# Key-page products on VectorE instead of GpSimd, in a one-core hybrid decoder step

## The chip, the cores and the metric

One core of a Trainium2 chip runs the whole program in one launch. The metric is the device time in microseconds (us), median of three runs.

## The reference, cut to what matters

One layer of a decoder serves a prompt of 512 tokens and a group of 8 samples, one token each, with the same weights. The normalised rows go through one wide projection `w_in`, whose columns feed four branches (a short gated convolution A, a gated DeltaNet B, a Conformer convolution C, a forgetting attention D); gated, merged and projected by `w_out`, they are followed by cross attention and a convolutional FFN. The change is in branch D of the samples: each of the 8 samples attends to 2048 cached tokens, kept as 16 pages of 128 tokens, 128 pages in all, found through a page table:

```python
s = jnp.einsum('bqhd,bkhd->bhqk', qi, k, preferred_element_type=F32) * (d ** -0.5)
s = s + jnp.swapaxes(ci, 1, 2)[..., None] - ck
```

With one query token per sample, the first line is, for each page of 128 tokens by 8 heads by 64 channels, an elementwise product with the sample's query row (512 numbers) and a sum over the 64 channels of each head.

## The kernel before

Every weight matrix is cut into pieces of 128 columns (`PIECES`). For each piece SyncE loads the weights (`weights`, four pieces ahead, ring of five), ScalarE rounds them to a high half `wh`, GpSimd subtracts to get the low half `rawl` (`split`, L762, two pieces ahead), and TensorE forms three products, high by high, high by low and low by high, into one of two PSUM buffers `pb`. A piece is run in two halves of 260 tokens. VectorE or ScalarE then empties the buffer (`evac`); the pieces of kind `gx` are convolved by VectorE in that step (L1519, L1536, L1542, L1522).

The order of the work is one list, `TIMELINE`, made in Python by `timeline()`. Every engine walks the same list and issues its own share of each event, in that order, so an event that one engine must wait for delays all that this engine has behind it. Between the halves of pieces the list holds side items (`SIDE`: softmax rows, DeltaNet chunks `gdn`, layer norm `cln`, page logits `dc`, `ds`, ...), and three background streams, dealt out a few at a time by `background(kind, n)`: 124 convolution taps of branch C (`tap`, VectorE, L1648), 128 key pages (`k`), and value pages (`v`). After each half piece the loop calls `background("tap", ...)` and then `background("k", ...)`, with n of 1 or 2. A stream whose counter is still `None`, or at its end, adds nothing. The side list has marks: at `("REDUCES",)`, just after the third DeltaNet chunk and before the page logits, `background("k", 10 ** 6)` puts all pages not yet dealt out into the list at one place, and `kend` behind them.

A key page goes through a ring of four buffers `kring`. At event `k` i SyncE waits for `page_free` of page i-1 and loads page i+3 (`page`, L700 and L701); GpSimd multiplies page i by the query row `qb` (`product`, L773), which it has itself fetched from DRAM at every sixteenth page (L770); VectorE sums page i-1 over the heads' channels (`reduce_page`, L1655). At `kend` GpSimd fetches the pages' forget gates (L784), and the side item `dc` 0 sums them on VectorE (L1528) for TensorE. Helpers `tt`, `stt`, `ts` on VectorE issue an operation and wait for it before the next one. `own_head`, `qscr`, `qs_out` are the head mask, the queries in DRAM and the semaphore of their store.

Of the kernel before, what the change touches and what calls it, by code (L numbers as in the profile page):

```python
# [22 lines left out]
P = 128  # L23
# [191 lines left out]
def timeline():  # L215

    out, pos, step_n, tile, at_piece, bg = [], [0], [0], [0], [-1], {"tap": None, "k": None, "v": None}
    size = {"tap": N_TAP, "k": N_PAGE, "v": len(V_EVENTS)}

    def background(kind, n):  # L220
        for _ in range(n):
            if bg[kind] is not None and bg[kind] < size[kind]:
                out.append(V_EVENTS[bg[kind]] if kind == "v" else (kind, bg[kind]))
                bg[kind] += 1

# [206 lines left out]
def build(nc, a, out):  # L432
    ctx = ExitStack()
    with ctx:
# [225 lines left out]
        @block.sync  # L660
        def _(sp):
            sp.dma_start(cst[:, 0:2 * P], a["cst"][:, 0:2 * P]).then_inc(id_in, 16)
            for t in range(QT):
                sp.dma_start(xrow[:, t, :], a["x_prompt"][0, t * P:(t + 1) * P, :]).then_inc(x_in, 16)
            sp.dma_start(xrow[0:NB, QT, :], a["x_sample"].rearrange("b t d -> (b t) d")).then_inc(x_in, 16)
            sp.dma_start(cst[:, 2 * P:], a["cst"][:, 2 * P:]).then_inc(par_in, 16)
            sp.wait_ge(pool_made.sem, 1)
            rows = [(V_MIX, "norm_mix"), (V_CROSS, "norm_cross"), (V_FFN, "norm_ffn"), (V_MEM, "norm_mem"),
                    (V_CB, "conf_dw_b"), (V_LG, "conf_ln_g"), (V_LB, "conf_ln_b"), (V_GN, "gdn_norm")]
            for at, name in rows:  # L670
                src = a[name].rearrange("l (r c) -> (l r) c", c=P)
                sp.dma_start(pv[at:at + src.shape[0], B_VEC, :], src).then_inc(par_in, 16)
            sp.dma_start(pv[V_FIN:V_FIN + 8, B_VEC, :], a["norm_final"].rearrange("(r c) -> r c", c=P)).then_inc(par_in, 16)
            for at, b, name in ((V_SW, B_VEC, "sconv_w"), (V_GW, B_VEC, "gdn_conv_w"), (0, B_CW, "conf_dw_w"),
                                (0, B_FW, "ffn_conv_w")):
                src = a[name].rearrange("l w (r c) -> (l w r) c", c=P)
                sp.dma_start(pv[at:at + src.shape[0], b, :], src).then_inc(par_in, 16)
            for b, n, name in ((B_SS, 1, "state_sconv"), (B_GS, 4, "state_gdn_conv"), (B_CS, 8, "state_conf_conv"),
                               (B_FS, 4, "state_ffn_conv")):
                src = a[name].rearrange("b l w (r c) -> (b l w r) c", c=P)  # L680
                m = src.shape[0] // n
                sp.dma_start(pv[0:m, b:b + n, :], src.rearrange("(n m) c -> m n c", n=n)).then_inc(par_in, 16)
            with nc.allow_non_contiguous_dma(reason="16 columns of w_in, and vectors read by all partitions"):
                sp.wait_ge(pool_made.sem, 2)
                sp.dma_start(bias[:, 0:4], a["gdn_dt_bias"].to_broadcast([P, 4])).then_inc(small_in, 16)
                sp.dma_start(bias[:, 8:16], a["fox_fbias"].to_broadcast([P, 8])).then_inc(small_in, 16)
                sp.dma_start(bias[:, 16:20], a["gdn_a_log"].to_broadcast([P, 4])).then_inc(small_in, 16)
            def weights(p):

                u, half = PIECES[p][:2]  # L690
                w, row, kt, c = UNITS[u]
                c += half * P
                if p >= RING:
                    sp.wait_ge(piece_done.sem, p - RING + 1)
                sp.dma_start(raw[:, p % RING, 0:kt, :], W[w][row:row + kt * P, c:c + P].rearrange("(k p) n -> p k n", p=P))\
                    .then_inc(raw_in[p % RING], 16)

            def page(cache, i, to, landed):

                n = sp.value_load(ptr_[0:1, i:i + 1], min_val=0, max_val=a[cache].shape[0] - 1)  # L700
                sp.dma_start(to, a[cache][bass.ds(n, 1)].rearrange("a p l h d -> (a p) (l h d)")).then_inc(landed, 16)  # L701

            def k_page(i):
                page("cache_fox_k", i, kring[:, i % 4, :], page_in[i % 4])

            def v_group(g):
                for i in range(VG * g, VG * g + VG):
                    page("cache_fox_v", i, v_slot(i), v_in[i % 8])

            for p in range(RING - 1):  # L710
                weights(p)
            sp.wait_ge(pt_in, 32)
            for i in range(3):
                k_page(i)
            for e in TIMELINE:
                if e[0] == "piece" and e[2] == 0 and e[1] + RING - 1 < NP_:
                    weights(e[1] + RING - 1)
                elif e[0] == "k" and e[1] + 3 < N_PAGE:
                    if e[1] >= 1:
                        sp.wait_ge(page_free.sem, e[1])  # L720
                    k_page(e[1] + 3)
                elif e[0] == "vstart":

                    sp.wait_ge(pe_s.sem, upto(pe_works, ITEMS.index(("dc", 1)) + 1))
                    sp.wait_ge(sp_lo.sem, KB)
                    v_group(0)
                elif e[0] == "v" and VG * (e[1] + 1) < N_PAGE:
                    if e[1] >= 1:
                        sp.wait_ge(v_used.sem, e[1])
                    v_group(e[1] + 1)  # L730

            sp.dma_start(out["sc_s"][:, 0, 0:SCW - 2], a["state_sconv"][:, 0, 1:]).then_inc(out_sem, 16)
            sp.dma_start(out["gc_s"][:, 0, 0:GCW - 2], a["state_gdn_conv"][:, 0, 1:]).then_inc(out_sem, 16)
            sp.dma_start(out["cf_s"][:, 0, 0:CFW - 2], a["state_conf_conv"][:, 0, 1:]).then_inc(out_sem, 16)
            sp.dma_start(out["ff_s"][:, 0, 0:FCW - 2], a["state_ffn_conv"][:, 0, 1:]).then_inc(out_sem, 16)
# [3 lines left out]
        def _(pool):  # L739
# [22 lines left out]
                pool.tensor_tensor(rawl[:, p % RING, 0:kt, :], raw[:, p % RING, 0:kt, :],  # L762
                                   wh[:, p % (AHEAD + 1), 0:kt, :].bitcast(F32), SUB).then_inc(lo.sem, 1)

            def product(i):

                if i % PAGES == 0:
                    if i == 0:
                        pool.wait_ge(qs_out, 16)
                    pool.dma_start(qb[:, :], qscr[i // PAGES:i // PAGES + 1, :].to_broadcast([P, 512])).then_inc(qb_in, 16)  # L770
                    pool.wait_ge(qb_in, 16 * (i // PAGES + 1))
                pool.wait_ge(page_in[i % 4], 16 * (i // 4 + 1))
                own(pool.tensor_tensor(kring[:, i % 4, :], kring[:, i % 4, :], qb[:, :], MUL), prod_done)  # L773

            for p in range(AHEAD):
                split(p)
            for e in TIMELINE:
                if e[0] == "piece" and e[2] == 0 and e[1] + AHEAD < NP_:
                    split(e[1] + AHEAD)
                elif e[0] == "k":  # L780
                    product(e[1])
                elif e[0] == "kend":
                    pool.wait_ge(page_free.sem, N_PAGE)
                    pool.indirect_dma_start(lf[:, :, :].rearrange("p a b -> p (a b)"), None,  # L784
                                            a["cache_fox_logf"].rearrange("n p l h -> n (p l h)"),
                                            bass.IndirectOffsetOnAxis(ap=ptc[:, 0:1], axis=0)).then_inc(lf_in, 16)
                elif e[0] == "side" and e[2] == ("x", 0):

                    pool.wait_ge(qs_out, 32)
                    pool.wait_ge(mt_act.sem, mt_a[mt_of("cq")])  # L790
                    pool.dma_start(qx[:, :, :].rearrange("p b n -> p (b n)"),
                                   qscr.rearrange("b n -> (b n)")[None, :].to_broadcast([P, NB * 512])).then_inc(q8_in, 16)
                    pool.wait_ge(q8_in, 16)
                    pool.wait_ge(mk_in, 16)
                    for b in range(NB):
                        kprod.by(pool.tensor_tensor(kvc[:, b, :, :], kvc[:, b, :, :], spread(qx[:, b, :], 2, 1), MUL))
# [713 lines left out]
        def _(dve):  # L1510
# [140 lines left out]

            def reduce_page(i):

                dve.wait_ge(prod_done.sem, i + 1)
                page_free.by(dve.tensor_reduce(sc[:, i, :], kring[:, i % 4, :].rearrange("p (h d) -> p h d", h=FH), AX, ADD))  # L1655

            def side(K, s):
# [282 lines left out]
            for e in TIMELINE:  # L1940
# [20 lines left out]
                    tap(e[1])  # L1961
                elif e[0] == "piece" and e[2] == 0 and e[1] + AHEAD < NP_:
                    split(e[1] + AHEAD)
                elif e[0] == "k" and e[1] > 0:
                    reduce_page(e[1] - 1)
                elif e[0] == "kend":
                    reduce_page(N_PAGE - 1)
                elif e[0] == "v" and e[1] % V_OF == V_OF - 1:
                    dve.wait_ge(v_used.sem, e[1] + 1)
                    v_rows.by(dve.tensor_tensor(vdiag.rearrange("p (h d) -> p h d", h=FH), s3.rearrange("p (h d) -> p h d", h=FH),  # L1970
# [39 lines left out]
```

## Time and profile before

| what | value |
|---|---|
| median of 3 runs | 1837.2 us (1836.98 to 1845.5) |
| profiled execution | 1836.28 us |
| its span in the trace | 1834.5 us |
| TensorE, VectorE, GpSimd, ScalarE busy | 84%, 50%, 35%, 30% of the span |
| granted TensorE clock, mean | 0.893 |

The span is the time between the first and the last instruction that the trace holds; the execution's own time is 1.8 us longer. Busy shares are means over stretches that differ: which engine is full must be read stretch by stretch. In the trace PE is TensorE, DVE VectorE, ACT ScalarE, POOL GpSimd, SP SyncE, and `ar` is one large buffer that holds most intermediate tiles, the key pages and the query row among them.

### The profile page before, as it was taken

How to read it: one execution, taken by the hardware profiler on the slowest of the kernel's cores; microseconds unless marked ns; L12 is line 12 of the kernel's file. 1: busy time of each engine (PE TensorE's matmuls, PEld its weight loads, DVE VectorE, ACT ScalarE, POOL GpSimd, SP SyncE). 2: the span in 40 equal slices, each digit the busy share in tenths (PEclk: the TensorE clock that was granted, in tenths of full speed). 3: DMA queues.
4: the chain of work that ended last, by engine and by line, in shares of the span. 5: the costliest groups of instructions: out<-in, count | busy, mean ns of one | idle time of the engine just before them, and what ended most of it. 6: DMA issues, size and time to landing. Idle time of an engine off the chain costs nothing. (4 is left out here: it accounts for less than half of the span.)

```text
span 1834.5 us, 28395 instructions
## 1 busy us (share of the span) xinstructions
PE 1545.2 (84%) x11127; PEld 1426.6 (78%) x11127; DVE 917.6 (50%) x1353; ACT 555.8 (30%) x893; POOL 643.9 (35%) x354
## 2 busy tenths in 40 slices
PE   4996577789796978999888879889577999999996
PEld 3896577579796977877666659888476999999995
DVE  4169887998956743113222232264425566663122
ACT  3322441112214212254222223444214333333222
POOL 1266544555664712222111104310402344443440
PEclk8898787899898989999889879999867999999998
DMA  7145323433353416447433106432312233332331
GB/s 213 48 132 155 110 81 98 134 103 114 110 149 104 129 51 199 143 146 227 119 110 116 41 13 195 131 92 81 121 46 75 81 93 93 93 93 77 96 99 47
DMA packets 250997, 199.86 MB, mean 109 GB/s; under 512 B 11620, under 2 KB 208797, under 8 KB 250456
## 3 DMA queue, kind: packets, MB, share of 16 engines
q1 hardware_dynamic: 234149, 169.47, 31.7%
q10 hardware_dynamic: 15723, 23.86, 3.8%
q0 software_dynamic: 992, 4.72, 0.7%
q8 instruction: 88, 1.44, 0.3%
q14 instruction: 45, 0.37, 0.1%
HBM read 187.89 MB, written 10.81 MB: 108 GB/s over the span
## 5 line engine op out<-in xcount | busy, mean ns | idle before, releaser
L762 POOL TENSOR_TENSOR rawl<-raw,wh 128x1024 fp32r<-128x1024 f32 (+2 forms) x196 | 428.6, 2188 | 1040.4 <-ACT wh L1145 1038.8
L802 PE MATMUL pb<-xh,wh 128*128 128x260 f32 x2176 | 649.9, 299 | 48.7 <-DVE xl L1516 22.6
L802 PE MATMUL pb<-xl,wh 128*128 128x260 f32 x2176 | 633.7, 291 | 0.0
L802 PE MATMUL pb<-xh,rawl 128*128 128x260 f32 x2176 | 632.0, 290 | 0.0
L802 PEld LDWEIGHTS pb<-xh,wh 128*128 128x128 f32 x2176 | 430.7, 198 | 65.9 <-issue 39.2
L802 PEld LDWEIGHTS pb<-xl,wh 128*128 128x128 f32 x2176 | 430.5, 198 | 0.7
L802 PEld LDWEIGHTS pb<-xh,rawl 128*128 128x128 f32 x2176 | 429.9, 198 | 0.0
L1145 ACT ACTIVATE wh<-raw 128x1024 fp32r<-128x1024 f32 (+2 forms) x208 | 201.6, 969 | 551.1 <-PE pb L802 521.7
L802 PE MATMUL sd<-ar 128*128 128x128 f32 (+5 forms) x1584 | 280.9, 372 | 96.2 <-DVE ar L1516 37.2
L802 PEld LDWEIGHTS sd<-ar 128*128 128x128 f32 (+4 forms) x1584 | 200.2, 199 | 142.0 <-issue 80.8
L773 POOL TENSOR_TENSOR ar<-ar 128x512 f32<-128x512 f32 x128 | 187.5, 1465 | 86.3 <-DMA ar<-in_cache_fox_k 58.5
L1648 DVE SCALAR_TENSOR_TENSOR ar<-xT,cols,ar 128x512 f32<-128x512 f32 x120 | 134.5, 1152 | 1.2
L802 PE MATMUL pb<-oh,wh 128*128 128x260 f32 (+1 forms) x384 | 123.4, 321 | 7.6 <-ACT ar L1145 5.1
L802 PE MATMUL pb<-ol,wh 128*128 128x260 f32 (+1 forms) x384 | 117.0, 305 | 0.0
L802 PE MATMUL pb<-oh,rawl 128*128 128x260 f32 (+1 forms) x384 | 116.8, 304 | 0.0
L806 PE MATMUL sd<-cst,ar 128*128 128x128 f32 (+7 forms) x359 | 64.2, 302 | 51.0 <-DVE ar L1516 26.4
L1655 DVE TENSOR_REDUCE ar<-ar 128x8 f32<-128x512 f32 x128 | 84.7, 677 | 39.6 <-POOL ar L773 38.9
L802 PE MATMUL pb<-hh,wh 128*128 128x260 f32 x352 | 100.0, 284 | 2.6 <-DVE hl L1516 2.6
L1145 ACT ACTIVATE ar<-ar 128x520 f32<-128x520 f32 (+8 forms) x71 | 41.6, 586 | 195.3 <-DVE ar L1542 166.9
L802 PE MATMUL pb<-hh,rawl 128*128 128x260 f32 x352 | 99.5, 283 | 0.0
L802 PE MATMUL pb<-hl,wh 128*128 128x260 f32 x352 | 99.3, 282 | 0.0
L802 PE MATMUL sd<-ar,cst 128*128 128x260 f32 (+7 forms) x132 | 43.9, 473 | 65.1 <-DVE ar L1720 27.7
(168 smaller groups left out, 1739.6 us busy)
## 6 DMA issues: line engine op xcount, KB each, us to landing
raw<-in_w_in SPq DMA_DIRECT2D x80, 512.0 KB, 4.1
ar<-in_cache_fox_k SPq DMA_DIRECT2D x128, 256.0 KB, 2.7
ar<-in_cache_fox_v SPq DMA_DIRECT2D x128, 256.0 KB, 3.1
raw<-in_w_ffn_in SPq DMA_DIRECT2D x44, 512.0 KB, 3.7
raw<-in_w_branch SPq DMA_DIRECT2D x32, 256.0 KB, 3.2
raw<-in_w_ffn_out SPq DMA_DIRECT2D x16, 512.0 KB, 3.9
ar<-in_cache_mem_k ACTq DMA_DIRECT2D x1, 4096.0 KB, 19.5
raw<-in_w_out SPq DMA_DIRECT2D x8, 512.0 KB, 3.9
```

Source lines behind the costliest of these rows:

```text
L762: pool.tensor_tensor(rawl[:, p % RING, 0:kt, :], raw[:, p % RING, 0:kt, :], wh[:, p % (AHEAD + 1), 0:kt, :].bitcast(F32), SUB).then_inc(lo ...
L773: own(pool.tensor_tensor(kring[:, i % 4, :], kring[:, i % 4, :], qb[:, :], MUL), prod_done)
L802: return pe.matmul(o, l, r, start=start, stop=stop, skip_group_check=True)
L806: return pe.transpose(o, i, ident[0:n, 0:n])
L1145: own(act.activation(o, i, f, **kw), st)
L1648: dve_c.by(dve.scalar_tensor_tensor(out=oC[:, c, 0:SEQ], in0=g[:, j - 1:j - 1 + SEQ], scalar=w[:, j - 1:j], in1=oC[:, c, 0:SEQ], op0=MUL, ...
L1655: page_free.by(dve.tensor_reduce(sc[:, i, :], kring[:, i % 4, :].rearrange("p (h d) -> p h d", h=FH), AX, ADD))
```

## The change

GpSimd's `product` goes, with its query fetch. VectorE multiplies page i itself and sums it in the same event `k` i (before, it summed page i-1 there). SyncE fetches the query rows: the first at `kstart`, the next ones at the last page of each sample, once VectorE has made that page's product. And `background` gets a flag `turned`, by which the list leaves out one call for pages at each change of sample.

```diff
+    turned = [False]
     def background(kind, n):
         for _ in range(n):
             if bg[kind] is not None and bg[kind] < size[kind]:
+                if kind == "k" and bg[kind] % PAGES == 0 and bg[kind] > 0 and not turned[0] and n < 10:
+                    turned[0] = True
+                    return
+                turned[0] = False
                 out.append(V_EVENTS[bg[kind]] if kind == "v" else (kind, bg[kind]))
                 bg[kind] += 1
...
+            def query(b):
+                sp.dma_start(qb[:, :], qscr[b:b + 1, :].to_broadcast([P, 512])).then_inc(qb_in, 16)
...
-                elif e[0] == "k" and e[1] + 3 < N_PAGE:
-                    if e[1] >= 1:
-                        sp.wait_ge(page_free.sem, e[1])
-                    k_page(e[1] + 3)
+                elif e[0] == "kstart":
+                    sp.wait_ge(qs_out, 16)
+                    query(0)
+                elif e[0] == "k":
+                    if e[1] + 3 < N_PAGE:
+                        if e[1] >= 1:
+                            sp.wait_ge(page_free.sem, e[1])
+                        k_page(e[1] + 3)
+                    if e[1] % PAGES == PAGES - 1 and e[1] + 1 < N_PAGE:
+                        sp.wait_ge(prod_done.sem, e[1] + 1)
+                        query((e[1] + 1) // PAGES)
...
-                pool.wait_ge(page_in[i % 4], 16 * (i // 4 + 1))
-                own(pool.tensor_tensor(kring[:, i % 4, :], kring[:, i % 4, :], qb[:, :], MUL), prod_done)
...
-                dve.wait_ge(prod_done.sem, i + 1)
+                if i % PAGES == 0:
+                    dve.wait_ge(qb_in, 16 * (i // PAGES + 1))
+                dve.wait_ge(page_in[i % 4], 16 * (i // 4 + 1))
+                tt(kring[:, i % 4, :], kring[:, i % 4, :], qb[:, :], MUL, prod_done)
                 page_free.by(dve.tensor_reduce(sc[:, i, :], kring[:, i % 4, :].rearrange("p (h d) -> p h d", h=FH), AX, ADD))
...
-                elif e[0] == "k" and e[1] > 0:
-                    reduce_page(e[1] - 1)
-                elif e[0] == "kend":
-                    reduce_page(N_PAGE - 1)
+                elif e[0] == "k":
+                    reduce_page(e[1])
```

The first place is VectorE's order among the `gx` pieces, right after the sixteenth page. Before, each piece's two taps (L1648) had a page sum (L1655) behind each of them, in front of the next tile's convolution:

```order
L1522 SCALAR_TENSOR_TENSOR ar<-ar 128x520
L1648 SCALAR_TENSOR_TENSOR ar<-xT,cols,ar 128x512
L1655 TENSOR_REDUCE ar<-ar 128x8
L1648 SCALAR_TENSOR_TENSOR ar<-xT,cols,ar 128x512
L1655 TENSOR_REDUCE ar<-ar 128x8
L1519 TENSOR_SCALAR ar<-ar,cols 128x520
L1536 SCALAR_TENSOR_TENSOR ar<-ar,cols 128x512
```

In the changed kernel (its line numbers are 3 higher here) there is no page work between the convolutions:

```order
L1525 SCALAR_TENSOR_TENSOR ar<-ar 128x520
L1651 SCALAR_TENSOR_TENSOR ar<-xT,cols,ar 128x512 x2
L1522 TENSOR_SCALAR ar<-ar,cols 128x520
L1539 SCALAR_TENSOR_TENSOR ar<-ar,cols 128x512
L1545 SCALAR_TENSOR_TENSOR ar<-cols,ar 128x8
```

What moved: page events 16 to 90, which stood from piece 12 to piece 44, are not there any more.

The second place is VectorE's order where `("REDUCES",)` stands, in the middle of piece 61: behind the last operation of the third DeltaNet chunk (L1765) and in front of the page gates' sum (L1528). Before, one page sum was left:

```order
L1765 SCALAR_TENSOR_TENSOR ar<-ar,sd 128x128 x4
L1655 TENSOR_REDUCE ar<-ar 128x8
L1528 TENSOR_REDUCE ar<-ar 128x8
L1516 TENSOR_TENSOR ar<-ar,cst 128x64
L1525 COPY ar<-sd 128x8
```

Now, first rows and last rows (L1519 with `ar<-ar` 128x512 is the new product, L1661 the page sum):

```order
L1771 SCALAR_TENSOR_TENSOR ar<-ar,sd 128x128 x4
L1519 TENSOR_TENSOR ar<-ar 128x512
L1661 TENSOR_REDUCE ar<-ar 128x8
...
L1519 TENSOR_TENSOR ar<-ar 128x512
L1661 TENSOR_REDUCE ar<-ar 128x8
L1531 TENSOR_REDUCE ar<-ar 128x8
L1519 TENSOR_TENSOR ar<-ar,cst 128x64
L1528 COPY ar<-sd 128x8
```

What moved: between L1771 and L1531 there stand 75 such pairs with nothing between them, one for page 53 and 74 for pages 54 to 127.

## Rows read from the trace of the kernel before

**Rows 1.** The page: part 2 (40 slices) for VectorE and the granted clock.
```profile
DVE  4169887998956743113222232264425566663122
...
PEclk8898787899898989999889879999867999999998
```

**Rows 2.** Busy us (instructions) of PE, PEld, DVE, ACT, POOL by stretch; clock, DMA share, GB/s.
```profile
95.00:135.00 40.00, 35.78 (x300) 35.57 (x300) 28.59 (x30) 10.01 (x12) 26.59 (x17) 1.00 0.43 125
135.00:271.00 136.00, 89.17 (x610) 84.87 (x611) 117.58 (x147) 50.69 (x67) 74.39 (x42) 0.81 0.41 119
271.00:356.00 85.00, 67.64 (x384) 60.35 (x384) 72.78 (x121) 10.59 (x14) 42.06 (x24) 0.76 0.35 103
356.00:517.00 161.00, 128.08 (x973) 125.70 (x973) 150.83 (x214) 35.17 (x60) 90.10 (x56) 0.89 0.39 116
517.00:601.00 84.00, 68.56 (x517) 66.77 (x516) 47.43 (x84) 31.09 (x51) 49.60 (x35) 0.92 0.41 123
601.00:661.00 60.00, 53.10 (x447) 52.21 (x445) 34.88 (x44) 13.97 (x20) 35.66 (x24) 1.00 0.41 119
```

**Rows 3.** VectorE's groups by shape, 90 to 660 us: busy us, mean ns, idle before.
```profile
L1648 DVE SCALAR_TENSOR_TENSOR ar<-xT,cols,ar 128x512 f32<-128x512 f32 x120 | 134.5, 1152 | 1.2
L1655 DVE TENSOR_REDUCE ar<-ar 128x8 f32<-128x512 f32 x128 | 84.7, 677 | 39.6 <-POOL ar L773 38.9
L1536 DVE SCALAR_TENSOR_TENSOR ar<-ar,cols 128x512 f32<-128x512 f32 x44 | 41.3, 938 | 0.6
...
L1761 DVE TENSOR_TENSOR ar<-ar,cst 128x512 f32<-128x512 f32 x15 | 15.2, 1017 | 0.0
...
L1740 DVE TENSOR_TENSOR ar<-ar 128x512 f32<-128x512 f32 x3 | 2.1, 692 | 0.9 <-ACT ar L1145 0.7
```

**Rows 4.** One line's instructions each, ns min/median/max: the taps, the page sums, the page products.
```profile
L1648 DVE SCALAR_TENSOR_TENSOR ar<-xT,cols,ar x120: 733/751/2897, 124.5 to 516.2; 128x512 f32<-128x512 f32 x120
...
L1655 DVE TENSOR_REDUCE ar<-ar x128: 666/676/689, 104.8 to 652.2; 128x8 f32<-128x512 f32 x128
...
L773 POOL TENSOR_TENSOR ar<-ar x128: 1260/1296/2239, 103.4 to 639.4; 128x512 f32<-128x512 f32 x128
```

**Rows 5.** Sums over 135 to 517 us: the taps (L1648), the products (L773), the weight halves (L762).
```profile
sum 382.00, DVE 126.15; mean DVE 42.05
...
sum 382.00, POOL 123.70; mean POOL 41.23
...
sum 382.00, POOL 81.22; mean POOL 27.07
```

**Rows 6.** VectorE in order of time, one `gx` tile: start us, us.
```profile
177.78 0.90 DVE L1519 TENSOR_SCALAR ar<-ar,cols 128x520 f32<-128x520 f32 x1
...
183.37 0.68 DVE L1655 TENSOR_REDUCE ar<-ar 128x8 f32<-128x512 f32 x1
183.97 0.74 DVE L1648 SCALAR_TENSOR_TENSOR ar<-xT,cols,ar 128x512 f32<-128x512 f32 x1
...
185.22 0.93 DVE L1519 TENSOR_SCALAR ar<-ar,cols 128x520 f32<-128x520 f32 x1
```

**Rows 7.** VectorE, then TensorE, in order of time where the page sums end.
```profile
652.16 0.68 DVE L1655 TENSOR_REDUCE ar<-ar 128x8 f32<-128x512 f32 x1
657.50 2.00 DVE L1528 TENSOR_REDUCE ar<-ar 128x8 f32<-128x1024 f32 x1 [4.66 <-DMA ar<-in_cache_fox_logf,ptc]
...
660.60 1.06 PE L802 MATMUL sd<-ar,cst 128*128 128x8 f32 x4 [3.83 <-DVE ar L1516]
```

**Rows 8.** Loads: KB each, median us to landing; the page loads' spread; two issues on SyncE in a row.
```profile
ar<-in_cache_fox_k SPq DMA_DIRECT2D x125, 256.0 KB, 2.7
...
ar<-q_scratch POOLq DMA_DIRECT2D x8, 256.0 KB, 3.5
...
DMA to landing us min/median/max: 2.4/2.7/8.1
...
576.89 1.45 SPq L701 DMA_DIRECT2D ar<-in_cache_fox_k  x2
```

More of the change, by code:

```diff
@@ L763, in split @@
                                    wh[:, p % (AHEAD + 1), 0:kt, :].bitcast(F32), SUB).then_inc(lo.sem, 1)
[L765 to L771, printed above, removed]
-                pool.wait_ge(page_in[i % 4], 16 * (i // 4 + 1))
-                own(pool.tensor_tensor(kring[:, i % 4, :], kring[:, i % 4, :], qb[:, :], MUL), prod_done)
             for p in range(AHEAD):
@@ L779, in _ @@
                     split(e[1] + AHEAD)
-                elif e[0] == "k":
-                    product(e[1])
                 elif e[0] == "kend":
```

## The prediction, made before the changed kernel had run

> **What bounds the kernel now.** I read the slices of the page first. Up to about 650 us VectorE stands at 7 to 9 tenths in most slices, later at 1 to 6, and the granted TensorE clock dips to 7 and 8 tenths in the same slices [rows 1]. Then the busy times of six stretches, cut at the pieces' starts: 95 to 135 us (pieces 6 to 11), 135 to 271 (the `gx` pieces 12 to 23), 271 to 356 and 356 to 517 (pieces 24 to 44, with the single-token DeltaNet work and most of two chunks), 517 to 601 and 601 to 661 (pieces 45 to 61). From 135 to 517 VectorE is busy 117.6 + 72.8 + 150.8 = 341 of 382 us and TensorE 285, at granted clocks of 0.81, 0.76 and 0.89; from 601 to 661 VectorE is busy 34.9 of 60 and TensorE 53.1 at 1.00 [rows 2]. So VectorE sets the pace up to 517 us, and TensorE with its chain of DeltaNet steps behind that.
>
> Next, why VectorE is full. Its largest groups are 120 taps of 1152 ns and 128 page sums of 677 ns, and it idles 38.9 us for GpSimd's products, nothing to speak of for the taps [rows 3]. The taps range from 733 to 2897 ns, with the median at 751; the sums never leave 666 to 689 [rows 4]. An operation with two operands in SBUF is thus held up by something, a sum with one is not. What holds it is GpSimd, busy in the same stretch with 123.7 us of products and 81.2 us of weight halves [rows 5]. The Trainium skill says so too (SBUF — State Buffer, Who interferes with whom): two SBUF inputs contend with GpSimd's reads, a `tensor_reduce` never does; the trace agrees.
>
> **What the change really does to the order.** The flag `turned` is cleared by every call of `background` that adds something, also by the calls for taps. At page 16 a call for pages sets it and returns; the next call is for a tap, which clears it; the next call for pages sets it again and returns. So no page is dealt out until the taps end, in piece 44. Pages 16 to 90, which were summed from piece 12 to 44, leave that stretch; from piece 45 to 61 the list now deals pages 16 to 53, where it dealt 91 to 127 (at the later changes of sample one call is skipped, as no tap clears the flag), and the bulk call at `("REDUCES",)`, which the test `n < 10` exempts, puts pages 54 to 127, 74 pages, in one block. The order rows show both places.
>
> **The sum, part by part.**
> First, pages 0 to 15 (95 to about 154 us). A product on VectorE costs 692 ns, the row of a 128x512 product within `ar` (three of them) [rows 3]: 16 x 0.69 = 11 us more. Against this, GpSimd's products no longer hold up VectorE's operations there, and its waits for them vanish; I take +3, between 0 and +11.
> Second, 135 to 517 us. Removed: 75 sums at their start-to-start distance of 183.97 - 183.37 = 0.60 us [rows 6], 45 us. Also removed: hold-ups by products. The 114 taps of the stretch took 126.2 us [rows 5] where 0.74 each would be 84, so 42 us of hold-up; the other operations with two operands add some 28, of which 44 convolution steps of 938 ns and 15 chunk products of 1017, where a free one takes about 740 and 692 [rows 3], are half. GpSimd's products have 123.7 / 204.9 = 60% of its time there [rows 5], so 42 us of the 70 go. Some of this comes back, since weight halves stay. VectorE then needs 341 - 87 = 254 us, and TensorE's 285 (less where its clock recovers) is the larger. Bounds of the gain: above, down to VectorE's 254 and its few latency waits, 115 us; below, if the ratio of busy to span that TensorE has from 517 to 661 (121.7 of 144, 85%) holds and its clock doesn't rise, 285 / 0.85 = 335, a gain of 47. By stages I take: the `gx` stretch, where a tile's pitch was 185.22 - 177.78 = 7.4 us with two sums and little hold-up [rows 6] and the stretch's mean is 136 / 12 = 11.3, to 102 (-34); 271 to 356 to 70 (-15); 356 to 517, where DeltaNet steps pass back and forth, to 137 (-24), near the rate of the chunk from 601 on. Together -73.
> Third, 517 to 661 us. 38 products more on VectorE, 26 us, in front of DeltaNet steps that TensorE waits for; VectorE idled 36.6 + 25.1 = 61.7 us there [rows 2], part of it for those products. +2, between -10 and +15.
> Fourth, the block at piece 61. One page costs VectorE the product (0.71 with its own wait) and the sum (0.60): 1.31; with the waits on loads I take 1.35. Are the loads fast enough? A slot of the ring is free after its sum; SyncE issues two pages in 1.45 us, so one in 1.1, and a page lands 2.7 us later in the median [rows 8]: (1.31 + 1.1 + 2.7) / 4 = 1.28 us per page with four slots, just under VectorE's own 1.31. So 74 x 1.35 = 100 us. At pages 64, 80, 96 and 112 the query row is only asked for once product 63 (and so on) is done, and SyncE's landing, 3 us or so after the issue (3.5 for GpSimd's [rows 8]), is behind one sum of 0.6 only: 4 x 3 = 12 us. At pages 16, 32 and 48 the gap in the list covers it. Block: 112 us. Bounds: 97 from VectorE alone; if loads landed as late as the slowest of before, 8.1 us [rows 8], 2.6 us per page, 194.
> What covers the block? Nothing. Before, VectorE ended the last sum at 652.8, waited 4.66 us for the forget gates and summed them, and TensorE, whose next work is the product of just that sum, had waited 3.83 us until 660.60 [rows 7]. TensorE's order has no piece between, so it is idle for the whole block, and so are the engines that feed it: queued behind VectorE's block are the page gates and the emptying of tile 61 on; behind SyncE's page loads stand the weights from piece 66 on, of which four pieces are already in the ring. The forget gates' fetch waits for page 127 and comes after, as before.
> GpSimd's 128 products and 8 query fetches are gone, and gain nothing beyond the hold-ups already counted: GpSimd was busy 35% of the span.
> Sum: 3 - 73 + 2 + 112 = +44, and +2 for TensorE's clock, low after so long a halt. The profiled execution took 1836.3 us (span 1834.5, 1.8 around it), 0.9 below the median: 1837.2 + 46 = 1883 us, 2.5% slower.
>
> **The rivals.**
> *The loads set the block's pace* (12 in 100). A page every 1.38 us or less is 190 GB/s, and 1.28 against 1.31 leaves nothing. With landings of 5 us the page takes 1.85: 137 + 12, so +83: 1920. For it: landings up to 8.1. Against it: the weights, which shared the queues, stop.
> *The stretch ahead gives less* (14 in 100): the DeltaNet chain and not VectorE holds it, gain 47: +72, 1909.
> *The stretch ahead pays for the block* (8 in 100, not slower). VectorE falls to its 254 us plus 13, and TensorE's clock, 0.76 to 0.89, rises towards 1.00, which shortens its 285 us. The gain is 115: 3 - 115 + 2 + 112 = +2, 1839 us. It decides from a gain of about 107 on. Against it: from 601 to 661, where VectorE is not full and the clock is 1.00, TensorE is still only 88% busy.
> *The pages are spread as before and the products merely change engine* (2 in 100). VectorE gets 128 x 0.69 = 88 us, loses hold-ups of about 50 (the 42 above and what lies outside that stretch) and 38.9 us of waits: -1, 1836. The order rows speak against it; the list decides. The Trainium skill (GPSIMD Engine Reference, 4.1 Engine selection) recommends just that, VectorE for an elementwise product with two inputs, GpSimd being about twice as slow; the trace agrees, 1296 ns against 692. By that rule alone the products cost half and the kernel is no slower.
>
> **How the numbers follow.** My forecast, +46 with its own range of 1858 to 1905, has 64 in 100. The range for 8 in 10 leaves out the two small cases near 1839 and below and the slow tail of the loads: 1854 to 1924. A measurement tells 0.5%, 9 us, from nothing. Slower by more: the forecast and the first two rivals, 64 + 12 + 14, and of the third rival none: 0.90. The third rival's 8 and the fourth's 2 split around zero: same 0.06, faster 0.04.
>
> **What the changed profile would show.** Right: in the 382 us stretch VectorE without page sums, pieces 12 to 44 done some 70 us sooner, taps with a mean nearer 0.95 us; then, at about 590 us, a hole of some 112 us in TensorE with VectorE alternating product and sum at a distance of 1.3 to 1.4 us, and four waits of about 3 us for `qscr`; behind it everything as before, only later. Wrong: a block with gaps between the pairs that end on page loads; a stretch ahead that is as long as it was, with TensorE waiting for ScalarE or for its own chain; or a block in which TensorE works.

## The result, and the profile after

The changed kernel takes 1905.5 us in the median (1903.1 to 1907.2, four runs) where the kernel before took 1839.1 beside it: a ratio of 1.0345, 95% interval 1.032 to 1.037, some 66 us slower. The forecast was 1883 us, slower by 46; the time lies half a microsecond above its own range of 1858 to 1905 and inside the wider one of 1854 to 1924.

The page of the changed kernel, its span and the 40 slices of TensorE, VectorE and the granted clock:

```profile
span 1902.8 us, 28270 instructions
...
PE   4986679789887005999889888998668899999996
...
DVE  5088677877698885412322223245233566664021
...
PEclk8898788999989557999888978999867899999998
```

Against [rows 1] two slices of 47.6 us, from 618 to 714 us, stand out: TensorE at 0 and 0, VectorE at 8 and 8, the clock at 5 and 5 tenths. That is the block of pages. Now the stretches, cut at the starts of the same pieces as [rows 2] (pieces 6, 12, 24, 30, 45, 52), and then the block; the columns are those of [rows 2]:

```profile
95.00:131.00 36.00, 35.70 (x300) 35.49 (x298) 27.35 (x36) 9.87 (x12) 12.55 (x6) 1.00 0.42 126
131.00:255.00 124.00, 89.41 (x608) 85.11 (x608) 97.41 (x138) 50.57 (x68) 30.08 (x13) 0.83 0.35 96
255.00:333.00 78.00, 65.27 (x387) 57.95 (x387) 59.43 (x107) 11.48 (x15) 18.59 (x8) 0.80 0.21 58
333.00:468.00 135.00, 118.21 (x968) 116.37 (x967) 109.63 (x173) 34.20 (x59) 32.51 (x15) 0.96 0.20 54
468.00:522.00 54.00, 45.84 (x358) 44.31 (x357) 35.35 (x58) 18.37 (x26) 13.70 (x7) 0.99 0.45 127
522.00:609.00 87.00, 77.64 (x604) 76.37 (x604) 73.88 (x113) 25.50 (x45) 18.09 (x10) 0.93 0.44 125
609.00:722.00 113.00, 0.00 (x0) 0.00 (x0) 92.35 (x143) 1.54 (x2) 2.13 (x2) 0.52 0.60 175
```

Pieces 12 to 44 take 124 + 78 + 135 = 337 us, where they took 382; from the start of piece 45 to that of piece 61 it is 134 us, as before (468.4 to 602.8 us in its trace, 517.0 to 650.8 in the one of before). In the block no matmul is run for 113 us. VectorE's groups by shape, 90 to 730 us, show what its operations cost: the taps, the products, the page sums, the convolution steps.

```profile
L1651 DVE SCALAR_TENSOR_TENSOR ar<-xT,cols,ar 128x512 f32<-128x512 f32 x120 | 118.4, 1034 | 1.2
L1519 DVE TENSOR_TENSOR ar<-ar 128x512 f32<-128x512 f32 x128 | 103.8, 811 | 36.3 <-DMA ar<-q_scratch 35.3 <-DMA ar<-in_cache_fox_k 0.2
L1661 DVE TENSOR_REDUCE ar<-ar 128x8 f32<-128x512 f32 x128 | 87.8, 686 | 4.4
L1539 DVE SCALAR_TENSOR_TENSOR ar<-ar,cols 128x512 f32<-128x512 f32 x44 | 32.9, 748 | 0.6
```

The taps fall from 1152 to 1034 ns only, and the products themselves take 811 ns where 692 is free [rows 3]; the convolution steps go all the way, from 938 to 748. The sums take 685 to 689, against 666 to 689 before [rows 4]: nothing holds them up in either kernel. The taps of pieces 12 to 44 together, to be set beside the 126.15 us of [rows 5]:

```profile
sum 337.00, DVE 113.94; mean DVE 37.98
```

VectorE in order of time where the block begins (page 53, then 54) and at the first change of sample in it:

```profile
604.10 0.69 DVE L1519 TENSOR_TENSOR ar<-ar 128x512 f32<-128x512 f32 x1
604.82 0.69 DVE L1661 TENSOR_REDUCE ar<-ar 128x8 f32<-128x512 f32 x1
605.42 0.68 DVE L1519 TENSOR_TENSOR ar<-ar 128x512 f32<-128x512 f32 x1
...
618.13 0.69 DVE L1661 TENSOR_REDUCE ar<-ar 128x8 f32<-128x512 f32 x1
622.43 0.69 DVE L1519 TENSOR_TENSOR ar<-ar 128x512 f32<-128x512 f32 x1 [3.61 <-DMA ar<-q_scratch]
```

Product, sum, product start 0.72 and 0.60 us apart: 1.32 us per page. Page 64 waits for its query row, from the end of a sum at 618.82 to 622.43. And the end of the block, VectorE in order of time, with TensorE's wait from 600 to 740 us (us in total, times, the longest):

```profile
718.89 0.69 DVE L1661 TENSOR_REDUCE ar<-ar 128x8 f32<-128x512 f32 x1
724.23 1.98 DVE L1531 TENSOR_REDUCE ar<-ar 128x8 f32<-128x1024 f32 x1 [4.65 <-DMA ar<-in_cache_fox_logf,ptc]
...
PE sd L805 <- DVE ar L1519: 117.9, 1, 117.9
```

The last sum ends at 719.6, the forget gates come 4.65 us later as before [rows 7], and TensorE has waited 117.9 us in one piece, where it waited 3.83. So the block costs it 114 us.

### The profile page after: what moved, and what is told of

The parts are those of the page before. It is cut to its first block and busy times, and to the rows that moved or that the text cites. A ratio compares the mean times of both kernels' runs of the same rounds, so it can differ in the third digit from the quotient of the medians.

```text
span 1902.8 us, 28270 instructions
## 1 busy us (share of the span) xinstructions
PE 1536.5 (81%) x11127; PEld 1417.6 (74%) x11127; DVE 963.0 (51%) x1481; ACT 555.9 (29%) x893; POOL 454.3 (24%) x218
## 5 line engine op out<-in xcount | busy, mean ns | idle before, releaser
L805 PEld LDWEIGHTS pb<-xh,wh 128*128 128x128 f32 x2176 | 425.8, 196 | 62.2 <-issue 33.4
L1148 ACT ACTIVATE wh<-raw 128x1024 fp32r<-128x1024 f32 (+2 forms) x208 | 201.6, 969 | 655.4 <-PE pb L805 627.2
L1519 DVE TENSOR_TENSOR ar<-ar 128x512 f32<-128x512 f32 (+6 forms) x183 | 150.2, 821 | 57.4 <-DMA ar<-q_scratch 35.3
L805 PEld LDWEIGHTS sd<-ar,cst 128*128 128x128 f32 (+2 forms) x132 | 29.6, 249 | 173.6 <-issue 131.2
L1651 DVE SCALAR_TENSOR_TENSOR ar<-xT,cols,ar 128x512 f32<-128x512 f32 x120 | 118.4, 1034 | 1.2
```

Source lines behind the costliest of these rows:

```text
L805: return pe.matmul(o, l, r, start=start, stop=stop, skip_group_check=True)
L1148: own(act.activation(o, i, f, **kw), st)
L1519: own(dve.tensor_tensor(o, x, y, op), st)
L1651: dve_c.by(dve.scalar_tensor_tensor(out=oC[:, c, 0:SEQ], in0=g[:, j - 1:j - 1 + SEQ], scalar=w[:, j - 1:j], in1=oC[:, c, 0:SEQ], op0=MUL, ...
```

## The experiments

Each ran beside the kernel before on its chip; ratios are to that kernel, with 95% intervals. Between chips the kernel before varied from 1839 to 1844 us, so kernels of different rounds are compared by their ratios or by the starts of pieces in their traces.

**Order or engine?** The first kernel repairs the flag and leaves all else as changed:

```diff
-                turned[0] = False
+                if kind == "k":
+                    turned[0] = False
```

> The changed kernel, but the flag is cleared only by calls for pages, so pages 16 to 127 are dealt out from piece 13 to piece 61, one call left out at each change of sample, and no block is left but the last five pages. Theory (the order, and not the engine, makes the loss): VectorE gets 128 products at a distance of 0.72 us, 92 us, and loses the hold-ups by GpSimd's products (50 to 58 us) and the 39 us in which it waited for them; with a few us more of hold-ups by the weight halves the time is 1835 to 1855 us. Rival (the products on VectorE cost their full time where VectorE is full, 75 x 0.72 = 54 us and more): 1885 us or above.

Measured: 1857.9 us, ratio 1.0076 (1.0043 to 1.0110). Pages 16 to 122 are spread again and most of the loss is gone: 0.0345 falls to 0.0076. The time is 3 us above the range given for the theory, and far from the rival's. What is left, 14 us, is the price of the engine and of the last five pages in piece 61. VectorE's products and taps in this kernel, by shape (its profiled execution, 1847.1 us, was the shortest of the six):

```profile
L1520 DVE TENSOR_TENSOR ar<-ar 128x512 f32<-128x512 f32 x128 | 133.7, 1045 | 22.9 <-DMA ar<-q_scratch 21.4 <-DVE ar L1520 0.8
L1652 DVE SCALAR_TENSOR_TENSOR ar<-xT,cols,ar 128x512 f32<-128x512 f32 x120 | 103.7, 897 | 1.2
```

A product takes 1045 ns in the mean in place of 692, so the 128 are held up for 45 us in all. They are not held up alike: 33 of them run at the same time as one of GpSimd's weight halves and take 2081 ns in the mean, the other 95 take 693 at most. The move doesn't end the contention; VectorE now suffers it in its own queue.

The second kernel does the reverse: the kernel before, engines and all, with only the list of the changed one.

```diff
+                if kind == "k" and bg[kind] % PAGES == 0 and bg[kind] > 0 and not turned[0] and n < 10:
+                    turned[0] = True
+                    return
+                turned[0] = False
```

> The kernel before, products and query fetches by GpSimd, with nothing changed but the list: the flag as in the changed kernel, so the same pages in the same places and the same block of 74 pages in piece 61. Theory (the order makes the loss): the stretch before the block is shortened by nearly the same 48 us, the block lasts 74 x 1.3 us of GpSimd's products and four query fetches of about 5 us, some 118 us: 1900 to 1915 us. Rival (the move to VectorE makes the loss): near 1840 us.

Measured: 1915.9 us, ratio 1.0374 (1.0342 to 1.0406), 1 us above the theory's range. The list alone makes the whole loss. Its stretches for pieces 12 to 44, columns as above, and TensorE's wait at the block:

```profile
134.00:257.00 123.00, 88.55 (x608) 84.28 (x608) 97.13 (x128) 52.35 (x69) 43.81 (x21) 0.85 0.35 95
257.00:336.00 79.00, 66.45 (x384) 59.08 (x385) 60.10 (x111) 11.15 (x15) 18.20 (x7) 0.78 0.21 56
336.00:470.00 134.00, 120.09 (x977) 118.24 (x976) 107.46 (x170) 34.73 (x60) 32.97 (x16) 0.95 0.21 55
...
PE sd L807 <- DVE ar L1521: 126.2, 1, 126.2
```

123 + 79 + 134 = 336 us, as in the changed kernel: which engine makes the products hardly matters there, since none is made after page 15, at about 153 us. The block holds TensorE up for 126.2 us with GpSimd's products, 8 us longer than with VectorE's. In the block, then, the engine chosen by the change is the better one.

**Does the gap at a change of sample do anything?** The changed kernel with the flag taken out:

```diff
-                if kind == "k" and bg[kind] % PAGES == 0 and bg[kind] > 0 and not turned[0] and n < 10:
-                    turned[0] = True
-                    return
-                turned[0] = False
```

> The changed kernel without the flag: pages are dealt out at every call, as in the kernel before, and no call is left out at a change of sample. Theory: as with the flag repaired (1835 to 1855 us), but VectorE waits up to 3.6 us at each of seven changes of sample, less what the taps and steps between the two pages cover: 5 to 20 us above the kernel with the repaired flag. Rival (the gap in the list isn't needed): within 4 us of it.

Measured: 1860.3 us, ratio 1.0082 (1.0050 to 1.0115), against 1.0076 with the repaired gap: no difference that can be told. The rival holds. In its trace VectorE waits 29.0 us for query rows in all, of which 19.2 is the first row; with the repaired flag it is 21.4, of which 19.1 is the first row. So the gaps do take away some 7 us of waits, but they also leave five pages for piece 61, which e11_no_rest below puts at some 4 us; that the two cancel is likely and not shown.

This kernel has exactly the list of the kernel before, and only the engine differs. So its 0.0082, 15 us, is the price of the engine alone.

**What sets the block's pace?** Only the first query row is fetched, and all pages are multiplied by it:

```diff
-                    if e[1] % PAGES == PAGES - 1 and e[1] + 1 < N_PAGE:
-                        sp.wait_ge(prod_done.sem, e[1] + 1)
-                        query((e[1] + 1) // PAGES)
...
-                if i % PAGES == 0:
-                    dve.wait_ge(qb_in, 16 * (i // PAGES + 1))
+                if i == 0:
+                    dve.wait_ge(qb_in, 16)
```

> The changed kernel with its first query row only: the seven later fetches and VectorE's waits for them are left out, so all pages are multiplied by the first sample's row. Theory (the four waits in the block, 15.5 us by the profile, add to VectorE's own 74 x 1.32 us): 1889 to 1892 us, 15 us less than the changed kernel. Rival (the loads set the pace, and the waits for query rows only give them time to catch up): 1900 us or above, with waits for page loads in the block.

Measured: 1887.4 us, ratio 1.0223 (1.0194 to 1.0253). TensorE's wait at the block, and VectorE's only wait for a page load there:

```profile
PE sd L802 <- DVE ar L1516: 102.2, 1, 102.2
...
DVE ar L1516 <- DMA ar<-in_cache_fox_k: 0.2, 1, 0.2
```

102.2 in place of 117.9 us, 15.7 less, as the theory had it, and the loads don't become the bound: VectorE waits for them once, 0.2 us. The block is VectorE's own work plus four waits for query rows. The time is 2 us below the range given for the theory, and by the ratios it is 22 us below the changed kernel; the intervals of the two allow 12 to 32, so the traces, with 15.7, are the better measure.

**Why did the stretch before the block give less than forecast?** In pieces 12 to 60 GpSimd fills the low half of the weights with zeros; the low product of these pieces is left out of the result, its matmuls are not.

```diff
+                if 12 <= p <= 60:
+                    pool.memset(rawl[:, p % RING, 0:kt, :].bitcast(F32), 0.0).then_inc(lo.sem, 1)
+                    return
                 pool.tensor_tensor(rawl[:, p % RING, 0:kt, :], raw[:, p % RING, 0:kt, :],
```

> The changed kernel, but for pieces 12 to 60 GpSimd fills the low half of the weights with zeros, which reads nothing, in place of the subtraction; the low product of these pieces is left out of the result, while TensorE does all its matmuls. Theory (in the stretch before the block VectorE is still held up by the subtractions, 24 + 11 + 15 us from piece 12 to 44): taps fall to a mean below 800 ns, and the start of piece 45 comes 20 to 45 us earlier than in the changed kernel: 1865 to 1885 us. Rival (the chain of TensorE, ScalarE and VectorE sets that stretch, hold-ups lie beside its waits): taps fall all the same, but piece 45 comes less than 10 us earlier, 1895 us or above.

Measured: 1864.1 us, ratio 1.0117 (1.0096 to 1.0138), 0.0228 or 42 us below the changed kernel. Piece 45 starts 36.0 us sooner than there, as the theory had it. Pieces 12 to 44 in three stretches; VectorE's products and taps by shape; the sum of the taps in these stretches:

```profile
132.00:240.00 108.00, 87.04 (x617) 83.30 (x616) 75.46 (x140) 50.72 (x67) 11.46 (x12) 0.87 0.40 108
240.00:304.00 64.00, 59.88 (x385) 52.77 (x384) 46.92 (x108) 11.22 (x14) 5.86 (x7) 0.87 0.26 71
304.00:432.00 128.00, 117.73 (x968) 116.78 (x967) 93.58 (x168) 33.95 (x59) 12.01 (x15) 0.96 0.21 57
...
L1522 DVE TENSOR_TENSOR ar<-ar 128x512 f32<-128x512 f32 x128 | 93.6, 731 | 35.4 <-DMA ar<-q_scratch 34.6
L1654 DVE SCALAR_TENSOR_TENSOR ar<-xT,cols,ar 128x512 f32<-128x512 f32 x120 | 83.9, 748 | 1.2
...
sum 300.00, DVE 79.38; mean DVE 26.46
```

The stretch takes 108 + 64 + 128 = 300 us, 37 less than in the changed kernel, though GpSimd still writes just as many elements (a fill of 1024 columns takes 0.95 us, a subtraction 2.2 to 2.4). The taps are at 748 ns, free: 33 of the 120 run at the same time as a fill, and the longest of all takes 754. So what holds VectorE up is GpSimd's reading of SBUF. That the low halves are ready sooner doesn't explain the gain, since TensorE waits for none of GpSimd's operations in this stretch, neither here nor in the changed kernel. The Trainium skill has the same rule (SBUF — State Buffer, Who interferes with whom): an operation of VectorE with two SBUF inputs contends with a GpSimd instruction that reads SBUF, not with one that only writes it.

**Can the pages be put where VectorE idles?** Three lists, none with pages in the `gx` pieces. The first two are edits of the kernel before, the third of the changed kernel with the repaired flag:

```diff
-            background("k", 1 if kind == "gx" or h == 0 else 1 + p % 2)
+            background("k", 0 if kind == "gx" else 2 if p >= 45 else 1 if h == 0 else 1 + p % 2)
```

> The kernel before with its own engines; only the list deals no pages during the gx pieces, 1 and 2 in turn up to piece 44 as before, and 2 a half piece from piece 45 on, so that page 127 stands in piece 60. Theory (a page costs where VectorE is full, about 0.6 us and its hold-ups, and nothing where VectorE idles, 62 us from piece 45 to 61): the gx stretch gives 15 us as in the changed kernel, pieces 45 to 61 give back less than 8: 1824 to 1834 us where the kernel before takes 1837 to 1840. Rival (the later pieces have no room: each page delays a DeltaNet step that TensorE waits for): 1837 us or above.

Measured: 1848.5 us, ratio 1.0044 (1.0024 to 1.0065), slower. The theory fell. Up to piece 45 the kernel is 17.6 us ahead of the kernel before, as expected, and from piece 45 to 60 it loses 24. VectorE's wait for products from 380 to 680 us in it:

```profile
DVE ar L1655 <- POOL ar L773: 52.0, 31, 5.2
```

At two pages a half piece GpSimd's products, 1.3 us each, come late, and VectorE, which walks its list in order, stands in front of a page sum with DeltaNet steps behind it that TensorE needs. Idle time in a stretch was not room: it was, at least in part, VectorE's waiting in a chain.

```diff
-            background("k", 1 if kind == "gx" or h == 0 else 1 + p % 2)
+            background("k", 0 if kind == "gx" else 2 if p >= 45 else 1)
```

> As the kernel with late pages, but with only 1 page a half piece from piece 24 to 44, so that eight pages are left for piece 61. Theory: 14 pages fewer in the full stretch, -0.64 us each, -9, and a block of 8 pages, which at GpSimd's 1.3 us each is +10: within 4 us of the kernel with late pages. Rival (a block costs more than its pages): 8 us above it.

Measured: 1858.9 us, ratio 1.0089 (1.0060 to 1.0118), 10 us above the kernel with late pages, so the rival's side. From the start of piece 61 to that of 62 it takes 29.4 us (10.7 with late pages): the block of 8 pages costs 19 us. In its trace VectorE makes eleven sums behind the last DeltaNet step, from 655.4 to 671.7 us, each behind a product of GpSimd. GpSimd had fetched the query row of page 112 at 640.3 us and waited 3.75 us for it, and when that step ended it still had to make the products of three pages that stand ahead of the block's eight.

```diff
-            background("k", 1 if kind == "gx" or h == 0 else 1 + p % 2)
+            background("k", 0 if kind == "gx" else 2 if p >= 45 else 1 if h == 0 else 1 + p % 2)
```

> The changed kernel with VectorE's products, with the repaired flag and the list of late pages (none in the gx pieces, 2 a half piece from piece 45 on; six left for piece 61). Theory (a product on VectorE costs 0.72 us plus hold-ups of 0.35 by the weight halves, where on GpSimd it held VectorE up for about 0.45): better than the kernel with the repaired flag alone by 5 to 15 us, 1840 to 1850 us, and worse than late pages with GpSimd's products by 8 to 20 us. Rival (with room from piece 45 on the engine makes no difference): within 4 us of it.

Measured: 1862.6 us, ratio 1.0104 (1.0080 to 1.0128). No better than the repaired flag alone, against the theory, and 14 us worse than late pages with GpSimd's products, as its second half said. In the trace pieces 45 to 59 take 144.6 us, where they take 126.2 with the repaired flag and 124.4 in the kernel before. So late pages cost there though no product comes late from another engine: GpSimd's lateness was not the whole reason. Late pages don't pay with either engine.

**If GpSimd's reads hold VectorE up, can VectorE take the weight halves too?** An option of the kernel names the kinds whose low half VectorE makes; pieces 12 to 67 are added, to the changed kernel with the repaired flag and to the kernel before:

```diff
-LOW_BY_DVE = ("kv", "cq")
+LOW_BY_DVE = ("kv", "cq", "gx", "ac", "ah", "ab", "gateA", "brA", "gateC", "brC")
```

> The changed kernel with the repaired flag, and the low halves of the weights of pieces 12 to 67 made by VectorE in place of GpSimd, 1.22 us for a piece of 1024 columns where VectorE already does it later on. Theory (holding VectorE up costs more than doing the work there: in the kernel with the repaired flag the products lost 45 us and the taps 18 us to the weight halves, the rest some 12, against 51 us of new work for pieces 12 to 60): 1825 to 1848 us, below the kernel with the repaired flag by 10 us or more. Rival (VectorE must now wait in its queue for ScalarE's high halves, and its page and DeltaNet work waits behind that): 1858 us or above.

> The kernel before, products by GpSimd, with only the low halves of pieces 12 to 67 made by VectorE. Theory: VectorE gets 51 us and loses 42 us of hold-ups by halves, but meets GpSimd's products more often: 1840 to 1860 us, so neither faster than before nor than the kernel with both on VectorE. Rival (products alone hold it up no more than before): below 1836 us.

Measured: 1832.2 us, ratio 0.9955 (0.9933 to 0.9978), with both on VectorE; 1839.2, ratio 0.9990 (0.9969 to 1.0011), with the halves alone, 1 us below the theory's range and not in the rival's. VectorE's products, taps and halves in the first of them:

```profile
L1520 DVE TENSOR_TENSOR ar<-ar 128x512 f32<-128x512 f32 x128 | 90.9, 710 | 20.4 <-DMA ar<-q_scratch 19.5 <-DVE cols L1529 0.3
L1652 DVE SCALAR_TENSOR_TENSOR ar<-xT,cols,ar 128x512 f32<-128x512 f32 x120 | 85.6, 747 | 1.2
L1635 DVE TENSOR_TENSOR rawl<-raw,wh 128x1024 fp32r<-128x1024 f32 x39 | 47.5, 1217 | 5.1 <-ACT wh L1149 4.9
```

The products fall to 710 ns and the taps to 747. VectorE makes 47.5 us of halves of 1024 columns and 91 us of products, yet the kernel is 0.0121, some 22 us, faster than the one with the repaired flag, and 8 us faster than the one before. With GpSimd's products kept, the halves alone bring nothing that can be told. Taking over one of GpSimd's two streams leaves the other to collide with; taking both frees VectorE.

Last, the five pages that the seven gaps had pushed into piece 61, spread before it; and with it the halves of pieces 4 to 11 too (`"cv", "cg"` added to the option):

```diff
-            background("k", 1 if kind == "gx" or h == 0 else 1 + p % 2)
+            background("k", 1 if kind == "gx" or h == 0 else 2 if p >= 45 else 1 + p % 2)
```

> The kernel with products and low halves on VectorE, and a list that deals 1 and 2 pages a half piece in turn from piece 45 on (1.5 in the mean, where it was 1.33), so that page 127 stands in piece 60 and no block of five pages is left in piece 61. Theory (a block is paid in full, 6.6 us from the start of piece 61 to that of 62, and five pages more in the pieces before cost less than half of that, since VectorE idles there): 3 to 6 us below the kernel with both on VectorE, 1826 to 1830 us. Rival (each page in front of a DeltaNet step delays it as much as the block does): within 2 us of it.

> As the kernel without the rest block, and the low halves of pieces 4 to 11 on VectorE too. Theory (hold-ups of some 10 us by six halves from piece 6 to 11, against 8 x 1.22 us of work, part of it while VectorE waits for the first query row): within 4 us of the kernel without the rest block. Rival (VectorE is late already at piece 12, so each microsecond taken away ahead of it counts): 4 us or more below it.

Measured: 1826.5 us, ratio 0.9933 (0.9908 to 0.9959), and 1825.6, ratio 0.9931 (0.9908 to 0.9955). TensorE's waits at piece 61 and just behind it, with the five pages there:

```profile
PE sd L806 <- DVE ar L1520: 10.5, 1, 10.5
PE sd L810 <- DVE ar L1520: 2.1, 1, 2.1
```

And without them:

```profile
PE sd L810 <- DVE ar L1520: 5.3, 1, 5.3
```

The wait of 10.5 us, for the sum of the page gates, is gone: with the last page in piece 60 the forget gates, too, are fetched while TensorE still works. A later wait grows from 2.1 to 5.3. The start of piece 62 comes 9.7 us sooner in the trace, though that of piece 61 comes 1.5 us later. By the ratios the time is 0.0022, 4 us, lower, less than the intervals can tell for sure. The halves of pieces 4 to 11 make no difference. These two are the shortest of the case, 0.7% below the kernel before.

## Why the prediction came out as it did

*The order.* Right, and it decided the sign. After page 15 the list deals no page up to piece 44, then 38 from piece 45 to 61 and 74 in the block, and e2_block_gpsimd shows that this alone makes the kernel 3.7% slower.

*The block, 112 us.* Right in each of its steps: 1.32 us per page (1.31 from the parts, 1.35 taken), no wait for loads but one of 0.2 us, the four changes of sample at about 3.9 us (3 taken), nothing that covers it. Measured 114 us; that it came so near 112 is in part luck, as the pages took 2 us less than forecast and the waits nearly 4 more.

*Pages 0 to 15, +3.* Piece 12 started 3.7 us sooner, not later, with nine of the sixteen products begun; the cost of the others lies in the next stretch and can't be told apart there. *Pieces 45 to 61, +2.* Measured +0.6 (piece 45 starts 48.6 us sooner than before, piece 61 48.0). *The clock, +2.* No run shows it. The start of piece 62 is 66.0 us later than before, that of piece 72 only 65.4. The last piece starts 68.3 us later, with 3 us picked up after piece 150, whose cause stays open. The parts read from the two traces add up as -3.7 - 44.9 + 0.6 + 114.0 + 2.3 = 68.3, where the medians differ by 66.5.

*Pieces 12 to 44, -73: the step that failed.* Measured 382 - 337 = -45. The step had two halves. VectorE's work was to fall by 87 us, 45 of sums and 42 of hold-ups; it fell from 341 to 266.5, by 75. The hold-ups were shared out by GpSimd's busy time, 60% to the products. That was too much for the products: of the taps' hold-up, the 126.2 us of 114 taps over the 79.4 that they take where nothing holds them (e5_zero_halves), 47 us, 33 were still there with the products gone (113.9 us for 116 taps). Matching the taps in the two traces with what GpSimd does at the same time shows why. Before, 39 of the 120 taps met a weight half, 22 of these a product as well, and they were held up for 33 us; 21 met a product only, for 16 us. In the changed kernel 40 met a half, for 35 us: what went is about the 16 us of the 21. The text said that some would come back and gave it no number. The other half weighs more: a fall of 75 us in VectorE's busy time moved the end by only 45, just under the lowest gain that the forecast allowed, 47. Stage by stage the forecast took -34, -15 and -24; measured were -12, -7 and -26. In the `gx` pieces and the single-token work the pitch of an unhindered tile was put in, as if what was left of the hold-ups lay beside the path. It lies on it: the same stretches go from 124 and 78 to 108 and 64 us once GpSimd reads nothing (e5_zero_halves). What makes up the rest of these stretches, among the waits of TensorE, ScalarE and VectorE for one another, no run takes apart. The second rival, less gain in the stretch ahead with 47 us, gave 1909 and was closest; its reason, the DeltaNet chain, was not the cause, since the stretch with the DeltaNet chunks was the one that gave what was forecast.

*The third rival* would have needed a gain of 107 us. Even without any reading by GpSimd, piece 45 starts 84.6 us sooner than before.

*The fourth rival*, products that only change engine, was put at 1836; e3_no_gap, which is just that, has it at +15 us over the kernel before, and e1_own_flag at +14. The sum there forgot that a product on VectorE has two SBUF inputs itself and is held up: 0.35 us in the mean, 45 in all (e1_own_flag).

## What to carry to other kernels

Where engines share one list, look first at what an edit does to the list: count the events stretch by stretch, before thinking about any instruction's price. Here work taken out of a full stretch gave back less than its busy time, 45 us for 75, while work put into one block in front of an operation that TensorE waits for cost its whole length. And where one engine holds another up through shared reads, moving half of its work may bring nothing: here the products moved alone cost 15 us, the halves alone gave 2, which can't be told from nothing, and both together gave 8.

## What the runs showed of the hardware

- GpSimd filling 1024 columns with a constant (0.95 us) held VectorE up not at all: taps of 748 ns in the mean and 754 at most (e5_zero_halves). GpSimd subtracting the same columns (2.2 to 2.4 us) left taps at 1034 ns in the mean (the changed kernel).
- The hold-up falls on whole operations. In the kernel before 60 of the 120 taps ran at the same time as an operation of GpSimd and took 1561 ns in the mean; the other 60 took 753 at most. The longest took 2897, some 2150 more than a free one, about the length of one weight half.
- The low half of a weight piece costs VectorE 1.22 us and GpSimd 2.2 to 2.4 us, and with GpSimd idle from 131 to 600 us VectorE's products stay within 3% of their free time (710 ns against 692), with VectorE 96% busy in one stretch of 135 us (e9_halves_vector).
- The page loads kept up with one page of 256 KB every 1.32 us (the core's DMA moved 195 GB/s in the mean) for 97 us with four buffers (e4_one_query).
- TensorE's granted clock was 0.52 in the mean in the block of 113 us without work, and 0.50, its lower level of 1.2 GHz, in each stretch of 10 us looked at from 620 us on. Piece 62 started 66.0 us later than before and piece 72 65.4, so the fall cost nothing that shows.
